# A decoder's sparse-attention layer: joined index weights, the sample's rows before tile 7, and stores that are waited for one stage later

## The reference

```python
def _odd_layer(x, pos, mk, mv, attend, norm_g, w_in, qn, kn, w_out, mem_qn):
    B, T, _ = x.shape
    xn = _rms(x, norm_g)
    q, k, v, g_c, qi, wi, ki, xq, g_x = _split(xn @ w_in, ODD_SPLITS)
    heads = lambda a, n: a.reshape(B, T, n, HEAD_DIM)
    q = _rope(_rms(heads(q, AT_HEADS), qn), pos)
    k = _rope(_rms(heads(k, AT_KV_HEADS), kn), pos)
    v = heads(v, AT_KV_HEADS)
    qi = _rope(qi.reshape(B, T, IDX_HEADS, IDX_DIM), pos)
    ki = _rope(ki[:, :, None, :], pos)[:, :, 0, :]
    wi = wi * IDX_HEADS ** -0.5
    yC = attend(q, k, v, qi, wi, ki).reshape(B, T, AT_W) * jax.nn.silu(g_c)
    yX = _mem_attn(heads(xq, XA_HEADS), mk, mv, mem_qn).reshape(B, T, XA_W) * jax.nn.silu(g_x)
    y = jnp.concatenate([yC, yX.astype(yC.dtype)], axis=-1) @ w_out
    return x + y.astype(x.dtype), (k, v, ki)

def _index_select(qi, wi, ki, qpos, topk):
    s = jnp.einsum('bqhd,bld->bqhl', qi.astype(jnp.float32), ki.astype(jnp.float32)) * IDX_DIM ** -0.5
    s = jnp.einsum('bqhl,bqh->bql', jax.nn.relu(s), wi.astype(jnp.float32))
    ...
    _, idx = lax.top_k(s, topk)
    return idx, idx <= qpos[None, :, None]
```

## Time and profile before

| | us |
|---|---|
| runs timed | 1904.47, 1905.33, 6233.31 |
| median | 1905.33 |
| profiled execution | 1901.79 |
| its span | 1900.2 |
| granted clock of TensorE, mean | 0.974 |

### The profile page before, as it was taken

The page is one execution under the profiler, slowest core; times in us unless marked ns, Lnnn a source line. Parts: engine busy times, 40 slices in busy tenths (PEclk is TensorE's granted clock), DMA queues, the critical chain, the costliest instruction groups (busy, mean ns, idle before and its releaser), DMA issues. The chain is left out here.

```text
span 1900.2 us, 26662 instructions
## 1 busy us (share of the span) xinstructions
PE 1793.1 (94%) x9489; PEld 1386.6 (73%) x9489; DVE 975.5 (51%) x2276; ACT 601.1 (32%) x1274; POOL 413.7 (22%) x646
## 2 busy tenths in 40 slices
PE   6999999999999998998999998999999679999999
PEld 5666888777788876886876566787667456777887
DVE  5513743234377665122432567888776675675111
ACT  3111332110022113101211346787634345553000
POOL 4301221000133352000341001211004265430000
PEclk9999999999899999999999999999999799999999
DMA  6334333553356468221222121334333674332331
GB/s 213 127 113 131 109 108 107 162 167 117 111 164 195 135 201 303 80 104 64 83 66 73 46 72 63 113 96 136 123 123 82 238 229 154 124 91 97 108 114 47
DMA packets 134350, 236.99 MB, mean 125 GB/s; under 512 B 28486, under 2 KB 60774, under 8 KB 134218
## 3 DMA queue, kind: packets, MB, share of 16 engines
q1 hardware_dynamic: 110506, 171.96, 28.0%
q0 software_dynamic: 17328, 56.24, 9.5%
q10 hardware_dynamic: 6384, 7.08, 1.1%
HBM read 169.05 MB, written 66.17 MB: 124 GB/s over the span
## 5 line engine op out<-in xcount | busy, mean ns | idle before, releaser
L1212 PE MATMUL layer_acc<-layer_w_hi,layer_xT_hi 128*128 128x512 f32 x640 | 263.3, 411 | 0.2 <-PE all_banks L1360 0.2
L1214 PE MATMUL layer_acc<-layer_w_hi,layer_xT_lo 128*128 128x512 f32 x640 | 254.4, 398 | 0.0
L1213 PE MATMUL layer_acc<-layer_w_lo,layer_xT_hi 128*128 128x512 f32 x640 | 253.9, 397 | 0.0
L2772 PE MATMUL front_acc<-front_w_hi,front_xT_hi 128*128 128x512 f32 x520 | 221.2, 425 | 15.4 <-DVE front_st L3250 5.3
L2773 PE MATMUL front_acc<-front_w_lo,front_xT_hi 128*128 128x512 f32 x520 | 208.6, 401 | 0.0
L2774 PE MATMUL front_acc<-front_w_hi,front_xT_lo 128*128 128x512 f32 x520 | 208.2, 400 | 0.0
L1212 PEld LDWEIGHTS layer_acc<-layer_w_hi,layer_xT_hi 128*128 128x128 f32 x640 | 122.6, 192 | 30.8 <-issue 5.9
L1213 PEld LDWEIGHTS layer_acc<-layer_w_lo,layer_xT_hi 128*128 128x128 f32 x640 | 122.0, 191 | 26.9 <-issue 2.6
L1214 PEld LDWEIGHTS layer_acc<-layer_w_hi,layer_xT_lo 128*128 128x128 f32 x640 | 121.7, 190 | 27.2
L2772 PEld LDWEIGHTS front_acc<-front_w_hi,front_xT_hi 128*128 128x128 f32 x520 | 100.2, 193 | 50.9 <-issue 9.2
L3096 ACT ACTIVATE front_index_rows<-odd_bias,front_candidate 128x1024 bf16<-128x1024 f32 (+3 forms) x128 | 124.8, 981 | 13.2 <-DVE front_candidate L3390 8.2
(11 more groups left out here) (669 smaller groups left out, 3621.3 us busy)
## 6 DMA issues: line engine op xcount, KB each, us to landing
all_w<-in_w_even POOLq DMA_DIRECT2D x80, 256.0 KB, 3.9
h_even<-layer_st SPq DMA_DIRECT2D x79, 256.0 KB, 2.2
all_w<-in_w_odd POOLq DMA_DIRECT2D x61, 256.0 KB, 3.5
h_odd<-front_st SPq DMA_DIRECT2D x56, 256.0 KB, 2.0
layer_scratch<-h_even SPq DMA_DIRECT2D x46, 256.0 KB, 3.1
all_scratch<-in_w_mem SPq DMA_DIRECT2D x32, 256.0 KB, 4.0
all_scratch<-h_even SPq DMA_DIRECT2D x32, 256.0 KB, 3.7
all_scratch<-x SPq DMA_DIRECT2D x14, 512.0 KB, 3.7
```

What stands on the lines that cost most here:

```text
L1212: T.matmul(out[0:rows, :], xh[:, kk, to], wh[:, r, :], start=(kk == 0), stop=False)
L1213: T.matmul(out[0:rows, :], xh[:, kk, to], wl[:, r, :], start=False, stop=False)
L1214: ins = T.matmul(out[0:rows, :], xl[:, kk, to], wh[:, r, :], start=False, stop=(kk == KC - 1))
L2772: T.matmul(out[0:rows, :], xh[:, k, to], wh[:, r, :], start=(k == 0), stop=False, skip_group_check=True)
```

## The change

Four edits:

1. **Index weights joined.** The high and low parts of the 72 columns of a step lie side by side (steps 0 to 3 in the spare slots of `w_hi`, steps 4 to 7 in those of `w_lo`), and `small(k)` is two matmuls: x high by both parts (144 columns) and x low by the high part (72 columns). VectorE's two copies become sums over the two halves (`tensor_reduce`). The conversion of these weights, one copy on ScalarE and one subtraction on VectorE, is two of each.
2. **The sample in front of tile 7.** From the second chunk on the units are tiles 0 to 6, the sample, tile 7 (`tile_at`).
3. **Last stores waited for later.** Tile 7 of the last chunk is evacuated into a buffer of its own (`c.vals[1]`, all_mem_vals) and its store signals `gate_last`, waited for in the next stage before the buffer is loaded again. The stores of new keys signal `k_last`, waited for in `load_qk` of the next stage.
4. **Row tile 1 first.** `preps` calls `load_qk(2)` ahead of `load_k(2)`.

```diff
...
         w_small = c.bias_smp[:, 0:KC * WK].rearrange("p (k n) -> p k n", k=KC)
-        wk = [t[:, RING - 2:RING, :].rearrange("p r n -> p (r n)")[:, 0:KC * WK].rearrange("p (k n) -> p k n", k=KC)
+        wk = [t[:, RING - 2:RING, :].rearrange("p r n -> p (r n)")[:, 0:KC * WK].rearrange("p (k j n) -> p k j n", j=2, n=WK)
               for t in (wh, wl)]
...
             return raw[q % RAW], (c.raw_in[q % RAW], 16 * (RAW_LOADS_EVEN + loads))
-        in_parts = lambda n: n >= T1 and n % T1 == T1 - 1
+        st_of = lambda n: c.vals[1][:, 0, :] if n == UNITS - 1 else st[(n - T1) % ST]
+        tile_at = lambda chunk, j: j if chunk == 0 or j < T1 - 2 else 2 * T1 - 3 - j
+        in_parts = lambda n: n >= T1 and n % T1 == T1 - 2
         by_dve = lambda n: ORDER[n // T1][1] or in_parts(n)
...
 
-            return sum(ORDER[m // T1][1] for m in range(T1 - 1, n + 1, T1))
+            return sum(ORDER[m // T1][1] for m in range(2 * T1 - 2, n + 1, T1))
...
 
-        unit_of = lambda chunk, t: T1 * chunk + t
+        unit_of = lambda chunk, t: T1 * chunk + tile_at(chunk, t)
...
                     sp.wait_ge(hrq, u + 1)
-                    sp.dma_start(to, c.qk[u][0:rows_in(t), QH * HD:QK]).then_inc(kst, 16)
+                    sp.dma_start(to, c.qk[u][0:rows_in(t), QH * HD:QK]).then_inc(c.k_last, 16)
                     yield
...
                 if n >= T1:
-                    chunk, t = divmod(n, T1)
-                    m = n - T1
+                    chunk, t = n // T1, tile_at(*divmod(n, T1))
+                    done = stored[(n - T1) % ST] if n < UNITS - 1 else c.gate_last
                     sp.wait_ge(*evacuated(n))
-                    sp.dma_start(c.h_odd[cols_in(t), CW * ORDER[chunk][0]:CW * ORDER[chunk][0] + CW], st[m % ST][0:rows_in(t), :])\
-                        .then_inc(stored[m % ST], 16)
+                    sp.dma_start(c.h_odd[cols_in(t), CW * ORDER[chunk][0]:CW * ORDER[chunk][0] + CW], st_of(n)[0:rows_in(t), :])\
+                        .then_inc(done, 16)
             follow(plan, UNITS, dense, amid, norm=loads_norm(), prep=stores_prep(), smp=loads_smp(), index=loads_first(), find=idle(),
                    mem=loads_mem(), cached=loads_cached(), qk=loads_qk(), copy=idle(), cached_copy=idle(), decide=idle())
-            for n in range(UNITS - ST, UNITS):
+            for n in range(UNITS - ST, UNITS - 1):
                 sp.wait_ge(*stored_by(n))
             sp.wait_ge(b_out, 16)
-            sp.wait_ge(kst, 32)
             sp.wait_ge(kp_in, 16 * 8)
...
             def half(n, side):
-                chunk, t = divmod(n, T1)
+                chunk, j = divmod(n, T1)
+                t = tile_at(chunk, j)
                 rows, to, out = rows_in(t), cols_in(t), psD[n % 2]
...
                 def small(k):
-                    extra = psA[0:rows, 512 * (t % 2):512 * (t % 2) + WK]
-                    T.matmul(extra, xh[:, k, to], wk[0][:, k, :], start=(k == 0), stop=False)
-                    T.matmul(extra, xh[:, k, to], wk[1][:, k, :], start=False, stop=False)
-                    return T.matmul(extra, xl[:, k, to], wk[0][:, k, :], start=False, stop=(k == KC - 1))
+                    extra, w = psA[0:rows, 512 * (t % 2):512 * (t % 2) + 2 * WK], wk[k // 4][:, k % 4]
+                    T.matmul(extra, xh[:, k, to], w.rearrange("p j n -> p (j n)"), start=(k == 0), stop=False, skip_group_check=True)
+                    return T.matmul(extra[:, 0:WK], xl[:, k, to], w[:, 0, :], start=False, stop=(k == KC - 1), skip_group_check=True)
                 for k in range(KC // 2 * side, KC // 2 * side + KC // 2):
...
                     r = q % RING
-                    if t == 0:
+                    if j == 0:
                         pe.wait_ge(split_d, q + 1)
...
                                        skip_group_check=True)
-                    if t == T1 - 1 and k < KC // 2:
+                    if j == T1 - 1 and k < KC // 2:
                         ins.then_inc(freed, 1)
...
             def dense(n):
-                chunk, t = divmod(n, T1)
+                chunk, t = n // T1, tile_at(*divmod(n, T1))
                 rows = rows_in(t)
...
                 if in_parts(n):
-                    ins = A(st[m % ST][0:SMP, :], psD[n % 2][SMP:2 * SMP, :], ACT.Copy)
+                    ins = A(st_of(n)[0:SMP, :], psD[n % 2][SMP:2 * SMP, :], ACT.Copy)
                     if not ORDER[chunk][1]:
...
                 if by_dve(n):
-                    A(st[m % ST][0:rows, :], psD[n % 2][0:rows, :], ACT.Tanh).then_inc(tanhs, 1)
+                    A(st_of(n)[0:rows, :], psD[n % 2][0:rows, :], ACT.Tanh).then_inc(tanhs, 1)
                 else:
-                    A(st[m % ST][0:rows, :], psD[n % 2][0:rows, :], ACT.Copy).then_inc(ev_a, 1)
+                    A(st_of(n)[0:rows, :], psD[n % 2][0:rows, :], ACT.Copy).then_inc(ev_a, 1)
...
                 act.wait_ge(small_in, 16)
-                A(wk[0], w_small, ACT.Copy).then_inc(whi, 1)
+                for n in range(2):
+                    ins = A(wk[n][:, :, 0, :], w_small[:, 4 * n:4 * n + 4, :], ACT.Copy)
+                ins.then_inc(whi, 1)
                 for q in EARLY_SLICES:
...
             def finished(n):
-                m, (chunk, t) = n - T1, divmod(n, T1)
+                chunk, t = n // T1, tile_at(*divmod(n, T1))
                 rows = rows_in(t)
                 dve.wait_ge(tanhs, evacuated(n)[1])
-                v = st[m % ST][0:rows, :]
+                v = st_of(n)[0:rows, :]
                 if not ORDER[chunk][1]:
...
             def dense(n):
-                chunk, t = divmod(n, T1)
+                chunk, j = divmod(n, T1)
+                t = tile_at(chunk, j)
                 rows = rows_in(t)
...
                     dve.wait_ge(parts, part(n))
-                    V.tensor_tensor(acc, acc, st[(n - T1) % ST][0:SMP, :], ALU.add).then_inc(whole, 1)
+                    V.tensor_tensor(acc, acc, st_of(n)[0:SMP, :], ALU.add).then_inc(whole, 1)
                 if chunk + 1 < len(ORDER):
                     q = KC * (chunk + 1)
-                    if 2 <= t < (6 if chunk else 4):
-                        slice_w(q + t - 2)
-                    if t == T1 - 1:
+                    if 2 <= j < (6 if chunk else 4):
+                        slice_w(q + j - 2)
+                    if j == T1 - 1:
                         if chunk == 0:
...
                         for k in range(KC // 2, KC):
-                            if k == KC - 2 and chunk:
+                            if k == KC - 2 and by_dve(n):
                                 finished(n)
...
                     at = 512 * (t % 2)
-                    link(V.tensor_copy(c.wi[0:rows, t, :], psA[0:rows, at:at + IH]))
+                    both = heads(psA[0:rows, at:at + 2 * WK], 2)
+                    link(V.tensor_reduce(c.wi[0:rows, t, :], both[:, :, 0:IH].rearrange("p j n -> p n j"), AX.X, ALU.add))
                     if t >= 2:
...
                         dve.wait_ge(ikt, t - 1)
-                    V.tensor_copy(ik[t % 2][0:rows, IH * ID:(IH + 1) * ID], psA[0:rows, at + IH:at + WK]).then_inc(wkd, 1)
-                if by_dve(n) and (t < T1 - 1 or chunk + 1 == len(ORDER)):
+                    V.tensor_reduce(ik[t % 2][0:rows, IH * ID:(IH + 1) * ID], both[:, :, IH:WK].rearrange("p j n -> p n j"), AX.X, ALU.add)\
+                        .then_inc(wkd, 1)
+                if by_dve(n) and (j < T1 - 1 or chunk + 1 == len(ORDER)):
                     finished(n)
...
                 dve.wait_ge(whi, KC // 2 + 1)
-                V.tensor_tensor(wk[1], w_small, wk[0], ALU.subtract).then_inc(wk_d, 1)
+                for n in range(2):
+                    ins = V.tensor_tensor(wk[n][:, :, 1, :], w_small[:, 4 * n:4 * n + 4, :], wk[n][:, :, 0, :], ALU.subtract)
+                ins.then_inc(wk_d, 1)
                 for q in range(KC // 2, KC):
...
                 t, u = PREP[p], p % 2
+                if p < 4:
+                    sp.wait_ge(c.k_last, 64)
                 if p >= 4:
...
             def preps():
-                load_k(2)
                 load_qk(2)
+                load_k(2)
                 load_value(0)
...
                             sp.wait_ge(stored[(i + 1) % 2], 16 * ((i + 1) // 2))
+                        else:
+                            sp.wait_ge(c.gate_last, 32)
                         sp.dma_start(gc[(i + 1) % 2], c.h_odd[cols_in(i + 1), O_GC:O_GC + QH * HD]).then_inc(g_in[(i + 1) % 2], 16)
...
         c.raw_in, c.early_in = X.pool_sem("raw_in", 4), X.pool_sem("early_w_in", EARLY // 2)
-        c.early_slices_in, c.x1_last, c.y_last = X.pool_sem("early_slices_in"), X.sem("x1_last"), X.sem("y_even_last")
+        c.early_slices_in, c.x1_last, c.y_last = X.pool_sem("early_slices_in"), X.sem("x1_then_k_last"), X.sem("y_even_then_gate_last")
+        c.k_last, c.gate_last = c.x1_last, c.y_last
         with Stage(nc, "even") as E:
```

6 lines of the change are left out of this document (3 added, 3 removed).

## The result

The changed kernel took 1884.89 us (median of 6 runs, 1882.66 to 1887.34), the one before 1903.99 beside it (median of 6, of which one, 6233.31, stands far out): ratio 0.9899, 95% interval 0.9883 to 0.9915, a gain of 19 us where 10 were forecast, and outside the range on its fast side. The profiled execution took 1886.33, its span is 1884.7.

A forecast was written before the change was run, and what follows sets the result against it. The prediction took TensorE to bound the odd layer's input projection where its index heads are projected; -7.0 - 1.15 - 1.1 - 1.0 = -10.25 took the median from 1905.33 to 1895.1 us, range 1889 to 1902.

The forecast's parts named there:

- A: Joined index weights in the odd layer's projection: one 0.11 us weight load fewer in each of 64 steps, -7.0 us.
- Rival 1: Removed weight load was hidden, or the 144 columns take its place: A gives 0, time 1902.1 us; chance 0.10.
- B: Sample in front of tile 7: stalls at chunk ends change by -0.4, -1.1, -1.0 and +1.35, sum -1.15 us.
- rival 4: More gain: shrinking stalls also lose a half-clock stretch (2.0 at one), D reaches -1.5, B -4: 1889.7 us; chance 0.10.
- C: Last stores waited for in the next stage: SyncE leaves the projection stage sooner, -1.1 us.
- D: Row tile 1 loaded first in the next stage: ScalarE's wait and TensorE's first stall end earlier, -1.0 us.
- rival 3: Next stage's start gives nothing: later page loads or the new wait cancel C and D, 1897.2 us; chance 0.17.
- Rival 2: Slower: the sample's two-engine evacuation costs 1.35 at each of 7 chunk ends, plus three half-clock pauses, 1911.7 us; chance 0.05.

The follow-up runs named there:

- d_only: The kernel before with only row tile 1 asked for ahead of the key pages: 1902.68 us against 1902.05, ratio 1.0003.
- a_only: The kernel before with only the index weights joined: 1896.92 us against 1903.04, ratio 0.9965.
- b_only: The kernel before with only the sample's unit moved in front of tile 7 in chunks 2 to 8: 1892.77 us against 1903.04, ratio 0.9943.

## Why the prediction was wrong

- **A** (-7.0): right in mechanism and place. The load sets the spacing, two remain of three, 0.10 us a step in the profile, -6.1 in the medians. Rival 1 is out. One reading was loose: the starts of the three small matmuls aren't 0.11 apart each (L2758 is followed after 0.04, and L2772 after 0.31 in place of 0.23); it is the loads that are, and the sum is the same. The rule behind rival 1, from the Trainium skill's "TensorE: Matmul & The Clock Gate", section "Step-by-step: what each phase is for" (the next weights load during the running matmul), holds here for 512 columns; in unit 1 the steps at 72 and 144 columns are set by the load, and the measurement decides.
- **B** (-1.15): this is the step that failed, by its size: -10.3. Its parts: at the 2nd chunk's end -0.4 was forecast and the stall only split (1.6 and 1.1 for 2.7); at the 3rd -1.1 came as -1.2, though not at the stall of 3.6, which was to shrink and stayed at 3.5; at the 6th -1.0 came as -2.4; at the 7th +1.35 came as +1.4 (4.9 to 6.3; ScalarE has two counts in front there, not three). What failed is the sentence "The remaining ends (4th, 5th) have no stall of weight: 0". The stalls of 2.3 and 2.2 us behind those ends are in the view that the forecast read, and they fell by 1.5 and 1.8. Their own releasers are a copy and a load, no evacuation; but both stand behind a find round, and that round held the splits and the addition. These parts make -5.5. The other 4.8 stood in no term of B; by the profiles their likely source is the parts at 1.2 GHz, which the shrunken stalls no longer brought.
- **The way in which B was costed** is the cause of the rest. It priced what leaves VectorE's order (0.6), and only at the 6th end that TensorE's short unit moved against a chain which two other engines run. Its bound of -4 for B left out even these 5.5.
- **The half clock.** The forecast gave the stretch at 1.2 GHz to rival 4 and to one stall. In the profile of before all three of the stalls that went were followed by one (0.83, 0.83 and 0.69 above): behind the last the difference grew from -16.0 to -18.9 within 17 us. That rival, at 0.10 and 1889.7, was the nearest: it had the direction and the clock, but one such stretch of 2.0 where the profile had three worth 6.1, and a gain of 1.5 from D that didn't come.
- **C** (-1.1): right, 1.17 by the two issues; the medians (-2.0, with no change inside the interval) neither show nor deny it.
- **D** (-1.0): nothing. The earlier load ended ScalarE's wait of 2.29, which is in neither d_only nor the changed kernel, and nothing of it is left in the time; the key pages behind it are the likely reason, as rival 3 had it for this edit.
- **Rival 2** (slower): its price of 1.35 came at the one end that it named as shown, and at no other.

With the measured parts, -6.1 - 10.3 - 1.2 + 0 = -17.6, against 19.1 for the whole; the difference is within the intervals.

## What to carry to other kernels

Where one engine walks a list of units and two others run a chain of rounds beside it, a short unit is a place where the first one gains on the chain: keep it away from the chain's heaviest round (here the one with four splits). List all stalls of the engine that bounds a stage, those that a copy or a load releases too, and go back from each through the queue of the releaser before giving an edit zero. Price a stall twice, as itself and as itself with a stretch at the lower clock, and look at the granted clock behind each stall of the profile that the forecast starts from. The wait that was moved over the stage's end was worth just what the end waited for it (1.1 and 1.17), and the load that was moved ahead gained nothing, though one wait fell: what is held back belongs in the sum too.

## What was not expected of the hardware

- Joining two matmuls of 72 columns into one of 144 saved a whole weight load and cost nothing: the 144 columns pass in 0.07 us (919.71 to 919.78), under the 0.11 that a load of 128 weight columns needs. In the sample tile, with loads of 32 columns, 72 columns pass in 0.04.
- The clock after equal stalls differed: after 3.1 us of waiting at the same place the granted clock over the next 11 us was 0.69 in one execution and 1.00 in another. Runs of a_only lay between 1891.0 and 1899.1 us, and its profiled one, without a half-clock stretch at any of its three stalls, was 1891.9. b_only, in which the three are under 1 us, lay between 1892.1 and 1893.7. That the clock makes the wider spread is argued, not shown.
